# Two-block model kernel: row passes joined at their seams, memory projection ahead of a tile's queries

## The reference, cut to what matters

```
for l in range(2):
    hn = rmsnorm(h, mix_norm[l])
    h = h + (pool_mixer(hn) if l == 0 else sparse_attn_hgrn_mixer(hn))
    h = h + memory_cross_attn(rmsnorm(h, xattn_norm[l]), mem_n, ...)   # k, v of the memory by wkv[l]
    h = h + peer_ffn(rmsnorm(h, peer_norm[l]), ...)
return rmsnorm(h, final_norm)

def peer_ffn(xb):                       # per block of 128 tokens
    s = scores of 8 heads x 2 halves over 128 sub keys each
    s1, i1 = top_k(s[0], 16); s2, i2 = top_k(s[1], 16)      # the "lists"
    top, pos = top_k(all 256 sums s1 + s2, 16)               # the "heads"
    eid = i1 * 128 + i2 at pos                               # the "keys": 128 row numbers a token
    g = softmax(top)                                         # the "gates"
    act = gelu(dot(xb, u[eid]))
    return sum over the 128 picks of g * act * v[eid]
```

## Time and profile before

| | |
|---|---|
| median of three runs | 2464.88 us |
| the profiled execution | 2470.63 us |
| its span | 2468.5 us |
| granted clock of TensorE, mean | 0.955 |
| busy: TensorE / VectorE / ScalarE / GpSimd | 85% / 58% / 32% / 39% |
| first gather; end of the last pass | 818.3 us; 2455 us |
| chain 1; memory; rest of pass 0 | 850 to 1021; 1021 to 1131; 1131 to 1249 us |
| chain 2 with pass 1 | 1249 to 1690 us |
| chain 3 with pass 2 | 1690 to 2132 us |

### The profile page before, as it was taken

How to read it: one execution, slowest core, us unless ns; L and a number is a source line. 1 busy time by engine, 2 the same in 40 slices (tenths; PEclk the granted TensorE clock), 3 DMA queues, 4 the chain that set the end, 5 groups by cost and what they waited for, 6 DMA issues and landing times.

```text
span 2468.5 us, 26155 instructions
## 1 busy us (share of the span) xinstructions
PE 2107.3 (85%) x8926; PEld 1356.1 (55%) x8926; DVE 1442.3 (58%) x3722; ACT 794.1 (32%) x1833; POOL 970.3 (39%) x693
## 2 busy tenths in 40 slices
PE   3899979998967789998789999988999998777776
PEld 3764759987856656653235655454565545433322
DVE  6354242126741876735576975568597656867755
ACT  1332234344311232323334243323334332333332
POOL 2630547788720223233433233322323332244442
PEclk9899989999979899999999999998999999899999
DMA  8446545556525899999999999999999999699997
GB/s 331 136 155 204 168 151 162 167 174 192 171 74 176 330 357 420 375 385 424 425 369 421 392 423 420 421 378 360 421 394 396 420 421 418 256 425 410 412 425 305
DMA packets 144374, 793.93 MB, mean 322 GB/s; under 512 B 16024, under 2 KB 18200, under 8 KB 77680
## 3 DMA queue, kind: packets, MB, share of 16 engines
q0 software_dynamic: 75792, 546.99, 54.1%
q1 hardware_dynamic: 68304, 245.22, 28.1%
q10 hardware_dynamic: 144, 0.05, 0.0%
HBM read 791.13 MB, written 1.06 MB: 321 GB/s over the span
## 4 chain that ended last, share of the span: by engine, by line
PE 51%; DVE 26%; DMA 15%; ACT 4%; issue 2%; POOL 1%; DVEq 0%; SPq 0%; ACTq 0%; POOLq 0%
PE banks L846 17%; PE banks L758 14%; PE banks L878 10%; DMA rows_b<-in_uv,p_eid 7%; DMA rows_c<-in_uv,p_eid 6%; DVE arena L1678 3%; PE banks L1028 2%; DVE rows_c L2110 2%; DVE rows_b L2110 2%; DVE arena L2110 2%; PE banks L915 2%; DVE arena L1684 2%; DMA W<-in_weights 2%; ACT arena L1333 2%; DVE st L1684 1%
## 5 line engine op out<-in xcount | busy, mean ns | idle before, releaser
L667 POOL TENSOR_TENSOR W_lo<-W,W_hi 128x1024 fp32r<-128x1024 f32 x160 | 391.1, 2450 | 189.4 <-ACT W_hi L1280 188.9
L846 PE MATMUL banks<-arena 128*128 128x512 f32 x768 | 369.5, 619 | 97.2 <-ACT arena L1339 96.8
L714 POOL DMA_INDIRECT arena<-in_uv,p_eid x192 | 215.2, 1121 | 602.0 <-PE banks L846 496.0
L846 PE MATMUL banks<-rows_b,arena 128*128 128x512 f32 x768 | 357.5, 603 | 41.4 <-ACT arena L1339 41.4
L1331 ACT ACTIVATE arena<-arena 128x2 f32<-128x2 f32 x256 | 52.1, 203 | 861.9 <-DVE arena L1684 860.9
L714 POOL DMA_INDIRECT rows_b<-in_uv,p_eid x192 | 216.3, 1127 | 275.5 <-PE banks L846 266.0
L2110 DVE SCALAR_TENSOR_TENSOR rows_b<-rows_b,H 128x1024 f32<-128x1024 f32 x192 | 233.1, 1224 | 150.9 <-DMA rows_b<-in_uv,p_eid 149.8
L2110 DVE SCALAR_TENSOR_TENSOR arena<-arena,H 128x1024 f32<-128x1024 f32 x192 | 233.0, 1226 | 112.4 <-DMA arena<-in_uv,p_eid 110.0
L846 PEld LDWEIGHTS banks<-arena 128*128 128x128 f32 x768 | 143.0, 196 | 279.6 <-issue 156.4
L846 PE MATMUL banks<-rows_c,arena 128*128 128x512 f32 x512 | 246.9, 627 | 52.1 <-ACT arena L1339 52.0
L846 PEld LDWEIGHTS banks<-rows_b,arena 128*128 128x128 f32 x768 | 144.3, 193 | 223.5 <-issue 163.3
(11 more groups left out here) (276 smaller groups left out, 2902.2 us busy)
## 6 DMA issues: line engine op xcount, KB each, us to landing
W<-in_weights SPq DMA_DIRECT2D x440, 512.0 KB
gain<-in_rows SPq DMA_DIRECT2D x7, 512.0 KB
gain<-in_rows POOLq DMA_DIRECT2D x6, 512.0 KB, 5.1
arena<-in_keys SPq DMA_DIRECT2D x3, 1024.0 KB, 9.5
arena<-in_uv,p_eid POOLq DMA_INDIRECT x192
rows_b<-in_uv,p_eid POOLq DMA_INDIRECT x192
arena<-in_rows POOLq DMA_DIRECT2D x1, 2048.0 KB, 17.3
rows_c<-in_uv,p_eid POOLq DMA_INDIRECT x128
```

Of the source, the lines that this page charges most:

```text
L667: po.tensor_tensor(W_lo[:, slot, :], W[:, (PARTS * n + part) % RAW_RING, :], W_hi[:, slot, :].bitcast(F32), ALU.subtract).then_inc(S_("lo_ ...
L714: po.indirect_dma_start(rows[slot], None, io[f"uv{l}"], bass.IndirectOffsetOnAxis(ap=p_eid[:, t, j:j + 1], axis=0))\
L846: mm = pe.matmul(banks[:, plan.bank(f"p_v{c}", b), :], diag[:, n % DIAGS, :], rows[slot][:, D + b * BLK:D + (b + 1) * BLK], start=j == 0, ...
```

## The change

**Counters and seams.** A new `lead(c)` stands at the end of each chain instead of the setting of `at` at the start of the next. On TensorE it claims pass c's banks, does group 0 and sets `at` to 2; on VectorE and ScalarE it sets `at` and does group 0. TensorE's `feed` is left as it is. On VectorE the sum to X is a function of its own, `add_rows`, called between groups 0 and 1 of the next pass. So the k-th call in a chain does, counted as above:

| | TensorE | ScalarE | VectorE |
|---|---|---|---|
| before | group k-2 | group k-1 | group k-1 |
| after, chains 2 and 3 | group k | group k | group k |
| after, chain 1 | group k | group k | group k+1 |

**Lists.** The last `top_lists` of a chain moves behind norm 7 of the next chain (chain 0's behind the first two groups; the last one's ahead of the final norm); `odd` then feeds 3 groups instead of 4. ScalarE waits for these lists before it takes `o_ik`. **Memory.** `memory` moves ahead of chain 1's `queries`, on the engines (VectorE's `feed(16)` with it), in the table of weight tiles and in the bank plan. `HEADS_AT` of pass 0 is spread from every 4 to every 8 groups. **SyncE.** `load_masks` is issued at tile `o_hi` instead of `o_ik`, and waits for the previous chain's last scores instead of its lists; odd tables of chain 2 and `next_gain(1)` change place likewise. The banks of pass c are planned before those of pass c-1 are released.

```
-HEADS_AT = [{(PK if c else 4) * (n - 1) + 3: n for n in range(1, PH // 2)} for c in range(len(CHAINS))]
+HEADS_AT = [{(PK if c else 8) * (n - 1) + 3: n for n in range(1, PH // 2)} for c in range(len(CHAINS))]
...
-                sp.wait_ge(S_("lists_ready"), (PH // 2) * c)
+                sp.wait_ge(pe_filled, plan.mark(f"p_s3.{c - 1}"))
+                sp.wait_ge(S_("lists_ready"), PH)
...
@@ TensorE
+            def lead(c):
+                begin(c)
+                weigh(0)
+                at[1] = LEAD
...
             for c, (l, t) in enumerate(CHAINS):
-                if c:
-                    begin(c - 1)
                 if l:
                     odd(c, t)
                 cross(c, l, t)
-                queries(c, l, t)
                 if c == 1:
                     memory()
+                queries(c, l, t)
                 if c:
                     drain()
-            begin(3)
+                lead(c)
             drain()
@@ ScalarE
+            def lead(c):
+                at[:] = [c, 0]
+                feed()
...
+                act.wait_ge(S_("lists_ready"), (PH // 2) * c)
                 take(o_c[:, t, :], f"o_ik.{c}", cut=slice(0, P + 8))
@@ VectorE, odd
                 norm1(c, 7, t)
-                feed(4)
+                after(v, f"p_s3.{c - 1}")
+                top_lists(CHAINS[c - 1][0], 3)
+                feed(3)
@@ VectorE, queries and the loop over chains
-                for n in range(PH // 2):
+                for n in range(PH // 2 - 1):
                     after(v, f"p_s{n}.{c}")
                     top_lists(l, n)
-                    if n < PH // 2 - 1:
-                        feed()
+                    feed()
...
                 if c:
                     drain()
-            at[:] = [3, 0]
+                lead(c)
+                if c:
+                    add_rows(c - 1)
+                feed()
+                if l == 0 and t == 0:
+                    after(v, "p_s3.0")
+                    top_lists(0, 3)
```

More of the change, by code:

```diff
@@ L63 @@
 DIAGS = 8
+LEAD = 2
 CHAINS = [(l, t) for l in range(2) for t in range(2)]
[L67 removed]
+HEADS_AT = [{(PK if c else 8) * (n - 1) + 3: n for n in range(1, PH // 2)} for c in range(len(CHAINS))]
 COLS = {}
@@ L202, in chain @@
     p.add(f"x_o.{c}", 2)
+    if c == 1:
+        p.add("x_k1", 4, "scalar")
+        p.add("x_v1", 4, "scalar")
     p.add(f"T6.{c}", 2, "scalar")
@@ L206, in chain @@
         p.add(f"p_s{n}.{c}", taker="scalar")
-    if c == 1:
-        p.add("x_k1", 4, "scalar")
-        p.add("x_v1", 4, "scalar")
 def make_plan():
@@ L246, in make_plan @@
         chain(p, c, l, t)
+        p.add(f"p_v{c}", 2, marks=0, hold=True)
         if c:
             p.release(f"p_v{c - 1}")
-        p.add(f"p_v{c}", 2, marks=0, hold=True)
     p.release("p_v3")
@@ L268, in tiles_in_order @@
         t += [(f"{name}.{c}", i) for name in ("x_q", "x_o") for i in range(2)]
-        t += [(f"p_q{n}.{c}", 0) for n in range(PH // 2)]
         if c == 1:
             t += [("x_k1", 1), ("x_k1", 3), ("x_v1", 1), ("x_v1", 3)]
+        t += [(f"p_q{n}.{c}", 0) for n in range(PH // 2)]
     return t
@@ L580, in tables @@
                     next_gain(0, norms_at(1, 5))
-                    next_gain(1, norms_at(1, 6))
                 elif stage == "o_ik.2":
-                    sp.wait_ge(S_("lists_ready"), PH)
+                    sp.wait_ge(pe_filled, plan.mark("p_s3.1"))
                     row(lb_row.rearrange("p a b -> p (a b)"), "gamma").then_inc(S_("odd_in"), 16)
@@ L586, in tables @@
                     row(kv_row, "kv_norm").then_inc(S_("odd_in"), 16)
-                    load_masks(2)
-                elif stage == "o_ik.3":
-                    load_masks(3)
+                elif stage in ("o_hi.2", "o_hi.3"):
+                    load_masks(int(stage[-1]))
+                elif stage == "o_hf.2":
+                    next_gain(1, norms_at(1, 6))
                 elif stage == "o_hq.2":
@@ L2383, in queries @@
                         top_gates(c, 0)
-                    if n < PH // 2 - 1:
-                        feed()
-                if c == 1:
-                    feed(16)
+                    feed()
             for c, (l, t) in enumerate(CHAINS):
-                if c:
-                    at[:] = [c - 1, 0]
                 if l:
@@ L2394, in _ @@
                 cross(c, l, t)
+                if c == 1:
+                    feed(16)
                 queries(c, l, t)
@@ L2397, in _ @@
                     drain()
-            at[:] = [3, 0]
+                lead(c)
+                if c:
+                    add_rows(c - 1)
+                feed()
+                if l == 0 and t == 0:
+                    after(v, "p_s3.0")
+                    top_lists(0, 3)
+            after(v, "p_s3.3")
+            top_lists(1, 3)
+            feed(2)
             norm1(3, 10, 0, "final_ready")
             drain()
+            add_rows(3)
             norm1(3, 10, 1, "final_ready")
```

11 lines of the change are left out of this document (4 added, 7 removed).

## The result

| | before | after |
|---|---|---|
| median of the timed runs | 2465.0 us | 2884.97 us |
| ratio | 1 | 1.1703 (95% interval 1.1683 to 1.1723) |
| profiled execution; span | 2470.63; 2468.5 | 2883.7; 2881.8 |
| granted clock of TensorE, mean | 0.955 | 0.911 |
| first gather | 818.3 | 818.4 |

The change makes the kernel 17% slower. Chains 2 and 3 lose 197 and 198 us, chain 1 loses 17, the last pass 1.

A forecast was written before the change was run, and what follows sets the result against it. Bound by TensorE's work and the gathers beside it, nearly equal. 2470.6 + 340 (chains 2 and 3) + 8 (chain 1) - 10 (seams) = 2809; the median lies 5.75 lower: 2803, say 2800, range 2550 to 2900.

The forecast's parts named there:

- The call counters: Chains 2 and 3: TensorE loses its one-group distance, engines take turns; 177 us of waits, +141 in a chain.
- levels: Decay levels of a chain: TensorE waits 4.8 us in each, 35 us for the eight.
- takes: Banks that ScalarE takes: its copy stands ahead of the group's weights, 2.4 us at 12 places, 28 us a chain.
- queries: Behind each p_s, copy, top_lists and dots delay TensorE: 6.4 us four times, 25 us a chain.
- The clock: Chains 2 and 3: weigh runs slower behind waits of 4 us or longer; +30 to +60 a chain, taken as 30.
- Chain 1: TensorE loses only its distance to ScalarE; with heads and memory together +8, between -8 and +20.
- The seams: Between passes: earlier first groups and later lists let GpSimd issue sooner; -3 a seam, -10 in all.
- "faster" rival: The seams join and the chains keep their pace, zero distance costing nothing: 2445 us, chance 0.10.
- SyncE: Chain 3's masks no longer block weights behind a list: -9 to 0, taken as 0.
- The memory's place and the heads: Chain 1: pass 0's picks every 8 groups and memory ahead of the queries, from -8 to +8.
- turns only where they close: Levels, queries and norms cost, takes and attention are covered, the clock recovers: 2555 us, chance 0.15.
- The clock stays down: TensorE never regains the full clock between waits, +100 to +120 a chain: about 2960 us, chance 0.06.

The follow-up runs named there:

- e1: The changed kernel with TensorE put back one group behind VectorE and ScalarE, all else as changed: 2450.62 us.
- e3: The kernel before with TensorE's feed one group forward and nothing else of the change: 2963.42 us.
- e8: The changed kernel with five zero-matrix products on TensorE in six decay levels of each of chains 2 and 3: 2846.13 us.
- e7: e1 with the memory behind the queries again and pass 0's heads every 4 groups, as in the kernel before: 2445.27 us.
- e9: e7 with the last top_lists of each chain back ahead of the sum to X instead of behind the next norm: 2460.73 us.
- e11: e7 with SyncE's masks and odd tables issued as in the kernel before: 2465.24 us.

## Why the prediction was right, and where it was not

The direction and the mechanism held: forecast 2800 (2550 to 2900), measured 2885, 15 us from the top of the range. Step by step:

- **The call counters.** Right. e1 undoes the loss with the distance, e3 makes it with the distance alone. Forecast were 177 us of waits in a chain in over 50 waits; there are 175.3 in 48. The terms: levels 35, in the profile 38; takes 2.4 us each, 2.0 to 2.4; queries 6.4 each, 6.7 to 6.8. That the sums agree within 2 us is partly luck: of waits of 1.8 to 2.4 us there are 22 outside the levels, 49 us (some of them in norms and attention), where I had 12 takes and 28 us, and behind the lists only 3, 20 us, where I had 37 with the heads; the other 15, at norms and in attention, are 68 us, where I had 77. The chains' other idle time, 9 us in chain 2 before, went to nothing, which I had not counted.
- **The clock.** Right in kind, too small: 30 us a chain, and TensorE's busy time grew by 62 and 59. The mis-sized step is "about 20 of the waits are 4 us or longer", with a price for those alone. 20 such waits there are in chain 2, and `weigh` takes 6.1 us behind them on the mean: 49 us in all, where I took 1.5 each. And 11 more, behind waits of 1.8 to 3.5 us, took 5.2 to 6.7 too, like the one behind 2.27 us above: 20 us that I had not counted. Some 6 of these 69 us the chain had before the change too. It shows in the level's period as well, for which I gave 10 to 11 us: it is 13.0 to 13.6, and e8, with the clock up, has 10.6. The Trainium skill's "TensorE: Matmul & The Clock Gate", under "What's actually happening", puts the ramp penalty under 1% of a typical kernel's span. That is no bound here, where the clock falls again behind some 30 waits of a chain: TensorE's busy time grew by 121 us in the two chains, 4% of 2885.
- **Chain 1.** +17, forecast +8 with bounds -8 and +20. e1 ends it 32 us earlier than the changed kernel: so much does the missing group of distance cost there, where I had 15, and the rest of the change gives 15 back.
- **The seams.** Forecast -10. In the changed kernel nothing of them is to be seen, as the gathers are not the limit there. With the distance kept e7 is 20 us faster, the number of my "faster" rival, but by luck: I had put it down to the pauses at the seams, and it lies at the start of pass 0. e9 shows that my sentence against the lists behind the norm was the wrong way round: with the lists ahead the kernel is 15 us slower. And the earlier trace rows is not the first gather of pass 1. The first eight are issued between 1233 and 1249 us, up to the sum to X, and the one with the 13.47 us is the ninth, which waits for the first row's slot:

```profile
1232.87 0.93 POOL L714 DMA_INDIRECT arena<-in_uv,p_eid  x1 [2.70 <-PE banks L846]
...
1248.90 0.93 POOL L714 DMA_INDIRECT rows_c<-in_uv,p_eid  x1 [0.78 <-PE banks L846]
```

In e7 this wait is 2.3 us and the one of the second seam 5.9 instead of 16.2. That the chains gain no more than 1 us by it, I read from the first gather of pass 2, before which GpSimd is idle for 11.9 us in e7 and for 5.5 before: the pause has moved.
- **SyncE.** I took 0 with bounds -9 and 0. e11 says 20 us in a kernel at full pace, when the lists stand behind the norm: I had priced the old waits in the old order, and not in the order in which the lists come later.
- **The memory's place and the heads.** Taken together as -8 to +8; +12 and -6 alone, +5.3 together.
- **The balance.** Of the 85 us between forecast and result 55 are the two chains (the clock gave 61 more than priced, the waits 8 less, 2 are rounding), 9 chain 1, 10 the seams' gain that didn't come, 1 the last pass, and 7 the distance of the profiled execution to the median, which was 5.75 before and is -1.3 after; 82 in sum, and 3 are the rounding of 2803 to 2800.

The rivals: "turns only where they close" (2555) would need free takes, and they cost 2.0 to 2.4 us each. "The clock stays down" (2960) did not come: 0.87. The "faster" one came true only once the distance was back.

## What to carry to other kernels

Where work is interleaved by hand over in-order engines, write down for each call which item each engine does, and keep every consumer at least one item behind its producers; a call counter that moves one engine by one place can cost more than all that the reordering gains. More distance is not better: from zero to one it gave 434 us here, from one to two it took 33. A wait on one engine for something that moves later has to be looked for on every queue: with the lists behind the norm, SyncE's weights stood behind them (e11).

## What the runs showed of the hardware

Products whose result is zero, put into the time in which TensorE waits, made a kernel 39 us faster, as the granted clock stayed up: 0.95 instead of 0.75 over 75 us of levels, and `weigh` 3.7 us instead of 6.0 to 6.7 (e8). And it is not single long waits alone that bring the clock down: in chain 2 of the changed kernel, with a granted clock of 0.87 on the mean, `weigh` took 5.4 us behind some waits of about 2.2 us and 3.7 behind others of the same length.
